# Weight buffers and activation operands of a two-block transformer kernel placed on opposite sides of 128-byte lines in SBUF

## The reference

```python
def conv_ffn(h, w_up, conv_w, conv_b, w_down):
    u = h @ w_up
...
    return (jax.nn.silu(gate) * val) @ w_down
...
        x = x + g2 * (jnp.square(jax.nn.relu(h2 @ w_ff1[l])) @ w_ff2[l])
```

## Time and profile before

| | |
|---|---|
| median of 3 runs | 1459.15 us (1457.88 to 1460.45) |
| profiled execution, its own time | 1458.23 us |
| its span | 1456.4 us, 25774 instructions |
| TensorE busy | 1384.4 us (95%), weight loads 1339.1 us (92%) |
| VectorE / ScalarE / GpSimd busy | 871.7 / 802.8 / 544.1 us |
| mean granted TensorE clock | 0.976 |
| DMA | 278.22 MB, mean 191 GB/s |

### The profile page before, as it was taken

How to read it: one execution, slowest core, us unless ns; L and a number is a source line. 1 busy time by engine, 2 the same in 40 slices (tenths; PEclk the granted TensorE clock), 3 DMA queues, 4 the chain that set the end, 5 groups by cost and what they waited for, 6 DMA issues and landing times.

```text
span 1456.4 us, 25774 instructions
## 1 busy us (share of the span) xinstructions
PE 1384.4 (95%) x11032; PEld 1339.1 (92%) x11032; DVE 871.7 (60%) x1047; ACT 802.8 (55%) x954; POOL 544.1 (37%) x249
## 2 busy tenths in 40 slices
PE   6999899998999979999999998999999999899997
PEld 5988899998899979999989997999988998899996
DVE  4874766755555567666658767444445876734443
ACT  4646577765676457777536544554324564454431
POOL 5000188886231337988606000664000600066300
PEclk8999999999999989999999999999999999999999
DMA  6343577777664466777624444555542544455550
GB/s 259 120 141 116 213 282 262 259 275 306 229 228 160 136 240 246 268 266 264 232 103 173 168 145 145 181 196 176 197 145 80 201 154 145 146 194 182 185 192 29
DMA packets 40002, 278.22 MB, mean 191 GB/s; under 512 B 4432, under 2 KB 4560, under 8 KB 8144
## 3 DMA queue, kind: packets, MB, share of 16 engines
q1 hardware_dynamic: 32976, 226.23, 44.4%
q10 hardware_dynamic: 6912, 50.33, 9.0%
HBM read 275.50 MB, written 1.05 MB: 190 GB/s over the span
## 4 chain that ended last, share of the span: by engine, by line
PE 86%; DVE 6%; ACT 3%; POOL 2%; issue 2%; DMA 0%; DVEq 0%; ACTq 0%; SPq 0%; POOLq 0%
PE bank L749 22%; PE bank L750 22%; PE bank L751 22%; PE bank L714 3%; PE bank L715 2%; PE bank L721 2%; DVE low L1432 2%; PE bank L963 1%; PE bank L733 1%; PE bank L734 1%; PE bank L735 1%; PE bank L770 1%; PE bank L783 1%; DVE h L1565 1%; ACT high L1079 1%
## 5 line engine op out<-in xcount | busy, mean ns | idle before, releaser
L1432 DVE TENSOR_TENSOR low<-raw,high 128x2048 fp32r<-128x2048 f32 (+4 forms) x222 | 511.1, 2305 | 308.7 <-ACT high L1079 306.1
L749 PE MATMUL bank<-op_high,low 128*128 128x256 f32 x1904 | 545.6, 287 | 3.3 <-DVE low L1432 3.3
L750 PE MATMUL bank<-op_low,high 128*128 128x256 f32 x1904 | 535.7, 281 | 0.0
L751 PE MATMUL bank<-op_high,high 128*128 128x256 f32 x1904 | 533.6, 280 | 0.0
L1079 ACT ACTIVATE high<-raw 128x2048 fp32r<-128x2048 f32 (+4 forms) x222 | 406.7, 1833 | 157.3 <-PE bank L751 146.1
L749 PEld LDWEIGHTS bank<-op_high,low 128*128 128x128 f32 x1904 | 358.3, 188 | 8.9 <-DVE low L1432 4.8
L750 PEld LDWEIGHTS bank<-op_low,high 128*128 128x128 f32 x1904 | 358.8, 188 | 2.8 <-issue 2.4
L751 PEld LDWEIGHTS bank<-op_high,high 128*128 128x128 f32 x1904 | 360.9, 190 | 0.0
L750 PE MATMUL bank<-act_low,high 128*128 128x256 f32 x864 | 243.8, 282 | 0.0
L749 PE MATMUL bank<-act_high,low 128*128 128x256 f32 x864 | 243.7, 282 | 0.0
L751 PE MATMUL bank<-act_high,high 128*128 128x256 f32 x864 | 242.8, 281 | 0.0
(11 more groups left out here) (288 smaller groups left out, 1908.3 us busy)
## 6 DMA issues: line engine op xcount, KB each, us to landing
raw<-stream SPq DMA_DIRECT2D x198, 1024.0 KB, 4.8
adaw<-ada ACTq DMA_DIRECT2D x48, 1024.0 KB, 6.1
raw<-stream SPq DMA_DIRECT2D x10, 768.0 KB, 4.8
raw<-stream SPq DMA_DIRECT2D x10, 512.0 KB, 3.6
x<-xT SPq DMA_DIRECT2D x1, 1024.0 KB, 5.1
out<-h SPq DMA_DIRECT2D x1, 1024.0 KB, 3.9
raw<-stream SPq DMA_DIRECT2D x2, 384.0 KB, 3.4
consts<-consts_d SPq DMA_DIRECT2D x1, 672.0 KB, 14.2
```

The costliest lines, as they stand in the source:

```text
L749: pe.matmul(o, wl[:, w], oh[:, k, :], start=one, stop=False, skip_group_check=True)
L750: pe.matmul(o, wh[:, w], ol[:, k, :], start=False, stop=False, skip_group_check=True)
L751: mm = pe.matmul(o, wh[:, w], oh[:, k, :], start=False, stop=end, skip_group_check=True)
L1432: dve.tensor_tensor(low[m % SPLIT][:, 0:w], raw[m % RAW][:, 0:w], high[m % SPLIT][:, 0:w], ALU.subtract).then_inc(S["low_ready"], 1)
```

## The change

Six weight buffers are allocated high first, then low, behind a pad of 64 bytes; the pads between high and low parts of the operands go, and new pads stand ahead of three pairs. No instruction, wait or shape changes.

```diff
-        high, low = [None] * SPLIT, [None] * SPLIT
-        for into, name, i in ((high, "high", 0), (high, "high", 2), (low, "low", 2), (None, "half0", 16), (low, "low", 0),
-                              (high, "high", 1), (None, "half1", 16), (low, "low", 1)):
-            if into is None:
-                sb(name, [P, i])
-            else:
-                into[i] = sb(f"{name}{i}", [P, CHUNK], F32R)
+        sb("line0", [P, 16])
+        high = [sb(f"high{i}", [P, CHUNK], F32R) for i in range(SPLIT)]
+        low = [sb(f"low{i}", [P, CHUNK], F32R) for i in range(SPLIT)]
...
+        sb("line1", [P, 16])
         OH = sb("op_high", [P, KB, TOK], F32R)
-        sb("half2", [P, 16])
         OL = sb("op_low", [P, KB, TOK], F32R)
...
+        f("line3", [P, 16])
         XH = f("mix_high", [P, KB, TOK], F32R)
-        f("half5", [P, 16])
         XL = f("mix_low", [P, KB, TOK], F32R)
...
         AH = f("act_high", [P, 22, TOK], F32R)
-        f("half4", [P, 16])
         AL = f("act_low", [P, 22, TOK], F32R)
...
         SQH = f("smallq_high", [P, 4, TOK], F32R)
-        f("half6", [P, 16])
         SQL = f("smallq_low", [P, 4, TOK], F32R)
         SCH = f("smallc_high", [P, 4, TOK], F32R)
-        f("half7", [P, 16])
         SCL = f("smallc_low", [P, 4, TOK], F32R)
...
+        f("line2", [P, 32])
         BH = f("act2_high", [P, 32, TOK], F32R)
-        f("half3", [P, 16])
         BL = f("act2_low", [P, 32, TOK], F32R)
```

## The result

The changed kernel takes **1448.12 us** (median of 6 runs, 1442.56 to 1453.95) against 1458.74 for six runs of the kernel before: a ratio of **0.993, interval 0.9906 to 0.9955**. It is faster, but by a quarter of what was forecast: 10.6 us, not 43.5, and outside the range. The profiled execution took 1450.23 us, 8.0 less than that of before, with a span of 1448.4. Its six runs also lie four times as far apart as those of before (11.4 us against 2.8).

What follows compares the result with a forecast made beforehand. TensorE's split matmuls were taken as the bound, 1121 us of the chain. Of these, 1051 us at full clock times 0.0414 saves 43.5: 1458.2 - 43.5 = 1414.7, plus 0.9 for the median, 1415 us; range 1405 to 1436.

Steps and rivals of the forecast that it cites:

- The bound: TensorE's split matmuls make 77.0% of the chain that ended last, 1121 us of 1456.4.
- the map and the pad arithmetic: Places of weights and operands modulo 128, from code sizes rounded to 32 bytes; after the change weights at 64, operands at 0.
- no placement would save anything: Reading of the skill's SBUF page that TensorE never waits on anyone: gain zero; the prediction went by the trace instead.
- So I take 113.5 for the changed kernel: 118.4 - 113.5 = 4.9 ns: Split matmuls drop from 118.4 ns to chunk 71's 113.5 ns, 4.14% each, 43.5 us over 1051 us.
- No effect: Rival: chunk 71's pace comes from something else in its stage, or the places were misjudged; 1459 us, chance 0.06.
- The mirror argument: Chunks 144 and 154, weight and operand places exchanged, both take 5.65 us, so exchanging sides should not matter.
- One near meeting already costs nearly all, the second and third add little: Feed-forward chunks with one to three operand-weight meetings at the same place modulo 128 run at 117.7 to 119.6 ns a matmul.
- The lower clock: 70 us at half clock, all taken as on the chain and given no gain, leaving 1051 of 1121 us to speed up.
- The waits: TensorE's waits: only 1.5 us of gain, from 276 to 312 us, might become longer waiting for GpSimd; left to the range.
- the first rival: Partly given back: GpSimd bounds both conv feed-forwards' stages, losing about 16 us of gain there; 1431 us, chance 0.12.
- slower: Rival: operand at 0 with weights at 64 is the costly meeting, three per triple; +71 us, 1530 us, chance 0.04.
- if only one class gained: Sign of being wrong: only chunks of one number modulo 3, which selects their weight buffers, speed up.

Runs made afterwards that it cites:

- near: Changed kernel with weights and operands all at multiples of 128 bytes: 1469.78 us, 1.0087 of the kernel before.
- low elsewhere: Changed kernel with low weights 192 and high weights 64 bytes past all operands modulo 256: 1426.59 us, 0.9793; run again 1429.97 us, 0.9812.
- mirror kernel: Changed kernel with the sides exchanged, weights at multiples of 128 bytes and operands 64 past them: 1446.31 us, 0.9928 of the kernel before.

## Why the prediction had the right sign and four times the size

**The bound, the map and the pad arithmetic** held. Placement matters with nothing else changed: near is 1.0087, the changed kernel 0.993 and low elsewhere 0.9812, with the same instructions. The page "SBUF — State Buffer" of the Trainium skill says in "Who interferes with whom" that TensorE shares its ports with no other engine and never waits on one; no run here contradicts that for other engines, but "no placement would save anything", which I drew from it, is refuted by these three ratios.

**The step that failed** is "So I take 113.5 for the changed kernel: 118.4 - 113.5 = 4.9 ns". The 113.5 came from chunk 71, 24 matmuls, and 68. It was read as the price list of one placement; it was one of two rhythms that this placement allows. In its place the runs show a mixture: 34% of triples at 340, 66% at 353, a mean of 116.30 ns a matmul. From 118.27 that is 1.97 ns a matmul where I put 4.9, 18.8 us in place of 43.5, so 24.7 of the 35.5 us between the forecast gain and the 8.0 of the profile. The prediction itself said that only 48 matmuls show it, and gave that doubt 0.06 as "No effect"; that the fast pace could come in some stages and not in others was in no case.

**The mirror argument** was right and didn't carry the conclusion: the mirror kernel is at 0.9928 like the changed one. That chunk 144 equals 154 says that the two sides are worth the same; both of them were in the slow rhythm, and nothing in them could tell how often an apart stream is fast. The reading "One near meeting already costs nearly all, the second and third add little" was the clue that I explained away: 117.7 was a second level, not the price of one meeting.

**The lower clock** was a second, smaller term that was off. I gave its 70 us no gain, and should have asked whether they stay 70: 54 more matmuls ran at that level, 5.2 us lost. **The waits** were costed at nothing but 1.5 us behind GpSimd. That wait grew by 0.24 us (0.93 to 1.17 at 308.29); others grew by 5 us in all, the weight split first. In the second profile of the kernel with 90% fast triples the pace term comes out at 42.5 us, within 1 us of my 43.5, and 13.8 of it are given back to these two; in the first it is 42.2, and the span gained 36.9. So even with the rhythm as forecast the gain would have been some 29 to 37 us.

**The rest held.** The changed kernel's VectorE row below is the 2.29 us of the earlier trace rows; the chain has 76.6% of split matmuls; GpSimd didn't become a bound (the first rival), although at 1431 it would have come nearer to the result; "slower" by a mirror that doesn't hold is refuted by the mirror kernel. Of the signs, chunks "5.44 to 5.46 us apart in every class" and medians of 276 ns for every operand failed, the wait at line 963 came to 1.17 us instead of 2, and "if only one class gained" was the wrong way to look: classes gained alike, stages didn't.

```profile
978.71 2.29 DVE L1425 TENSOR_TENSOR low<-raw,high 128x2048 fp32r<-128x2048 f32 x1 [3.36 <-ACT high L1072]
```

**Open.** Why a given start falls into one rhythm, and why low weights 192 past the operands beside high ones 64 past favour the fast one, their exchange less and with a third pace, and both at 192 hardly; no run looks into the engine. Why the clock fell in the broken stages, in fast and slow streams. And how far the rhythms of one kernel differ from run to run: only the changed kernel and low elsewhere have two profiles.

## What to carry to other kernels

A pace that a few dozen instructions show may be one of several that a stream can hold: before it is multiplied by the length of a kernel, look whether the same code in another layer runs at the same pace, and give a chance to a mixture. When TensorE alternates weights and operands in fp32r at this rate, it is worth placing weight buffers 64 bytes off the operands modulo 128, and worth trying the low and high ones 128 bytes apart from each other: 0.7% and 1.9% here, for pads of some hundred bytes. And a faster bound does not bring all that its pace promises: in the two profiles where the pace gained 42 us, the span gained 37 and 29, so look at the clock row and the waits before the sum is believed.

## What the runs showed of the hardware that was not expected

- A stream of 256-column fp32r matmuls, each with its own weights, runs at 340 or 353 ns for three in the changed kernel, hardly anything else (1% of triples). With high weights 192 and low ones 64 past the operands 22% of the triples last 357 ns or more. 32 or 96 bytes between the sides modulo 128, or none, gives stage means of 350 to 360 and never 340.
- The rhythm survives the border between two chunks and two operands, 31 chunks long, and a single extra matmul of 32 to 128 columns can switch it for the next 48 matmuls; the same nudges gave the same sequence in both layers.
- The fastest triple anywhere is 339 to 340 ns, 113.3 a matmul. The Trainium skill's TensorE: Matmul & The Clock Gate, "Back-to-back issue gap", gives N / 2.4 + 2.5 ns for an isolated matmul, which as an estimate from that page is 109.2 ns for 256 columns; no run shows that here.
- A stage with faster matmuls got longer: 83.70 us at a granted clock of 1.00 before, 86.40 at 0.94 with mostly fast triples. But 87.00 at 0.96 in a kernel with none, so the faster matmuls are not shown to be the reason.
